# Decoder step on one core: conditioning rows turned by VectorE, position products as 16 products behind the third page unit, pages transposed two units ahead

## The reference

```python
def adaln(c, w_ada, b_ada):
    mod = jax.nn.silu(c) @ w_ada + b_ada
    return jnp.split(mod[:, None, :], 6, axis=-1)

def compress(rows, pe, w1, w2):
    ...
    proj = jnp.einsum('bnkf,rfh->rbnkh', chunks, w1.reshape(r_n, CMP_STRIDE * HEAD_DIM, CMP_HIDDEN))
    pre = sum(proj[r][:, r:r + nc] for r in range(r_n)) + pe.reshape(-1) @ w1
    out = jax.nn.silu(pre) @ w2
```

## Time and profile before

| | us |
|---|---|
| median of 3 runs | 924.52 |
| lowest and highest | 923.3, 925.25 |
| the profiled execution | 924.75 |
| its span, first to last instruction | 922.9 |
| PE busy in the span | 854.2 (93%) |
| DVE busy | 622.8 (67%) |
| ACT busy | 372.8 (40%) |
| POOL busy | 307.5 (33%) |

### The profile page before, as it was taken

The page is one execution under the profiler, slowest core; times in us unless marked ns, Lnnn a source line. Parts: engine busy times, 40 slices in busy tenths (PEclk is TensorE's granted clock), DMA queues, the critical chain, the costliest instruction groups (busy, mean ns, idle before and its releaser), DMA issues.

```text
span 922.9 us, 17110 instructions
## 1 busy us (share of the span) xinstructions
PE 854.2 (93%) x6689; PEld 733.0 (79%) x6689; DVE 622.8 (67%) x1219; ACT 372.8 (40%) x751; POOL 307.5 (33%) x303
## 2 busy tenths in 40 slices
PE   3498999999988789899999998999999999999998
PEld 2366778899976556676777798999999999888886
DVE  2156585388945775758486899888888888434444
ACT  1033252141234343767843664444444446223221
POOL 6465400000003321535500318777766773000000
PEclk9699999999988788999999999999999999999999
DMA  7988913236276798294102453333333324422201
GB/s 207 344 306 313 317 47 99 94 110 243 68 263 249 277 376 301 51 316 138 36 1 92 129 147 107 98 101 104 95 93 93 93 92 153 156 92 92 74 1 52
DMA packets 89166, 138.88 MB, mean 150 GB/s; under 512 B 9267, under 2 KB 59987, under 8 KB 84798
## 3 DMA queue, kind: packets, MB, share of 16 engines
q1 hardware_dynamic: 74866, 96.26, 32.6%
q0 software_dynamic: 9376, 40.31, 12.2%
q10 hardware_dynamic: 4844, 1.21, 0.6%
HBM read 130.58 MB, written 11.31 MB: 154 GB/s over the span
## 4 chain that ended last, share of the span: by engine, by line
PE 78%; DVE 8%; issue 7%; ACT 3%; another core or an unknown queue 1%; POOL 1%; DVEq 0%; ACTq 0%; POOLq 0%
PE bank L2438 18%; PE bank L2440 18%; PE bank L2439 18%; PE bank L2432 4%; PE bank L2506 4%; PE bank L2794 2%; PE bank L2708 2%; PE bank L2926 2%; PE bank L2467 2%; PE bank L2448 2%; PE bank L2447 2%; PE bank L2958 2%; PE bank L2764 1%; DVE mem L1602 1%
## 5 line engine op out<-in xcount | busy, mean ns | idle before, releaser
L2438 PE MATMUL bank<-s,ring_hi 128*128 128x288 f32 x620 | 184.7, 298 | 3.7 <-DVE ring_lo L536 3.7
L2439 PE MATMUL bank<-s,ring_lo 128*128 128x288 f32 x620 | 183.6, 296 | 0.0
L2440 PE MATMUL bank<-s,ring_hi 128*128 128x288 f32 x620 | 183.0, 295 | 0.0
L2438 PEld LDWEIGHTS bank<-s,ring_hi 128*128 128x128 f32 x620 | 116.8, 188 | 4.6 <-DVE ring_lo L536 4.5
L2440 PEld LDWEIGHTS bank<-s,ring_hi 128*128 128x128 f32 x620 | 117.5, 190 | 0.0
L2439 PEld LDWEIGHTS bank<-s,ring_lo 128*128 128x128 f32 x620 | 117.0, 189 | 0.0
L536 DVE TENSOR_TENSOR ring_lo<-mem,ring_hi 128x512 fp32r<-128x512 f32 x84 | 106.3, 1301 | 2.1 <-POOL mem L988 1.8
L536 DVE TENSOR_TENSOR dn_w<-wring,dn_w 128x2048 fp32r<-128x2048 f32 (+1 forms) x11 | 23.1, 2096 | 65.9 <-ACT dn_w L533 65.9
L2438 PE MATMUL bank<-dn_w,dn_hi 128*128 128x512 f32 x160 | 62.2, 389 | 0.0
L2439 PE MATMUL bank<-dn_w,dn_lo 128*128 128x512 f32 x160 | 62.2, 389 | 0.0
L2440 PE MATMUL bank<-dn_w,dn_hi 128*128 128x512 f32 x160 | 62.2, 389 | 0.0
(11 more groups left out here) (444 smaller groups left out, 2126.5 us busy)
## 6 DMA issues: line engine op xcount, KB each, us to landing
wring<-in_w_gu SPq DMA_DIRECT2D x44, 512.0 KB
wring<-in_w_ada SPq DMA_DIRECT2D x16, 1024.0 KB
wring<-in_w_in SPq DMA_DIRECT2D x10, 1024.0 KB
wring<-in_w_down SPq DMA_DIRECT2D x10, 1024.0 KB
wring<-in_w_ada SPq DMA_DIRECT2D x16, 512.0 KB
proj<-in_x_prompt SPq DMA_DIRECT2D x4, 512.0 KB
mem<-in_state_k_win POOLq DMA_DIRECT2D x8, 256.0 KB
mem<-in_state_v_win POOLq DMA_DIRECT2D x8, 256.0 KB, 7.5
```

What stands on the lines that cost most here:

```text
L2438: pe.matmul(dst, sh, ml, start=first and k == 0, stop=False)
L2439: pe.matmul(dst, sl, mh, start=False, stop=False)
L2440: ins = pe.matmul(dst, sh, mh, start=False, stop=last and k == len(pairs) - 1)
```

## The change

It does five things.

1. The conditioning rows are loaded in 8 DMAs so that four groups of partitions hold a quarter each (`crow` is 128 by 256 now, cleared by DVE ahead of the load), and after the Silu DVE transposes them in one instruction into `cT`. The 8 products on PE and the copy out of PSUM are gone.
2. The position products use both halves of the weight rows at once: 16 products with 128 columns of weights and two moving columns. DVE adds the two halves that are wanted (a copy and an addition for each of keys and values).
3. On PE the order is unit 0, unit 1, the transpose of the gain rows, unit 2, the position products, and only then `compress_second(0)`. All through the loop `compress_second` stands one unit later: unit u is followed by `compress_second(u - 2)`.
4. DVE transposes pages 0 and 1 ahead of its loop, and in iteration u page u + 2. That page's buffer is the one that PE frees when it has finished unit u.
5. On ACT's queue the loads of the value weights and of the second weights stand ahead of the gain rows.

The diff, cut to its core (the bank list `plan_banks` follows the new order on PE and loses the key `cT`; two semaphores, `c_cleared` and `c_turned`, are new):

```diff
@@ SP
-            sp.dma_start(crow[0:1, :], a["c_prompt"]).then_inc(c_loaded, 16)
-            sp.dma_start(crow[1:9, :], a["c_sample"]).then_inc(c_loaded, 16)
+            sp.wait_ge(c_cleared, 1)
+            for q in range(4):
+                for r0, n, name in ((0, 1, "c_prompt"), (1, 8, "c_sample")):
+                    sp.dma_start(crow[32 * q + r0:32 * q + r0 + n, :].rearrange("b (k r) -> b k r", r=32),
+                                 a[name].rearrange("b (k q r) -> q b k r", q=4, r=32)[q]).then_inc(c_loaded, 16)
@@ ACT
             hidden_load(0)
+            hidden_load(1)
+            for x, w in enumerate(("w_ck2", "w_cv2")):
+                act.dma_start(w2[:, 64 * x:64 * x + 64], a[w][0]).then_inc(comp_w_loaded, 16)
...
-            hidden_load(1)
-            for x, w in enumerate(("w_ck2", "w_cv2")):
-                act.dma_start(w2[:, 64 * x:64 * x + 64], a[w][0]).then_inc(comp_w_loaded, 16)
             act.dma_start(stc, a["state_conv"].rearrange("l b r f -> (l b r) f")).then_inc(conv_state_loaded, 16)
-            act.wait_ge(c_loaded, 32)
+            act.wait_ge(c_loaded, 128)
             act.activation(scrow, crow, ACT.Silu).then_inc(scrow_ready, 1)
@@ def hidden(u), ACT
+                if u < 2:
+                    want_emptied(act, ("peb", u))
@@ DVE
             turn_chunks(0)
+            turn_chunks(1)
             for u in range(16):
-                if u < 15:
-                    turn_chunks(u + 1)
-                if u >= 2:
-                    cmp_evac(u - 2)
-                if u == 0:
-                    evac(("cT",), cT[:, :].rearrange("p (k r) -> p k r", r=32)[:, :, 0:9],
-                         ps(("cT",))[:, 0:72].rearrange("p (k r) -> p k r", r=9))
+                if u < 14:
+                    turn_chunks(u + 2)
+                if u >= 3:
+                    cmp_evac(u - 3)
+                if u == 1:
                     evac(("rows",), colT[:, :], ps(("rows",))[:, 0:52])
+                    dve.wait_ge(scrow_ready, 1)
+                    dve.transpose(cT[:, :], scrow).then_inc(c_turned, 1)
                     for x in range(2):
-                        evac(("peb", x), pebt[:, x:x + 1], ps(("peb", x))[64 * x:64 * x + 64, 0:1])
+                        want_filled(dve, ("peb", x))
+                        link(dve.tensor_copy(pebt[:, 2 + x:3 + x], ps(("peb", x))[64:128, 1:2]))
+                        frees(dve.tensor_tensor(pebt[:, x:x + 1], pebt[:, 2 + x:3 + x], ps(("peb", x))[0:64, 0:1], ALU.add),
+                              ("peb", x))
...
+            cmp_evac(13)
             cmp_evac(14)
@@ def position_rows(), PE
                 for x in range(2):
                     want_free(pe, ("peb", x))
-                ins = [None, None]
-                for i in range(16):
-                    for x in range(2):
-                        ins[x] = pe.matmul(ps(("peb", x))[64 * x:64 * x + 64, 0:1], w1v[:, x, i % 8, i // 8, :], colT[:, 36 + i:37 + i],
-                                           start=i == 0, stop=i == 15)
-                for x in range(2):
-                    fills(ins[x], ("peb", x))
+                    for j in range(8):
+                        ins = pe.matmul(ps(("peb", x))[:, 0:2], w1v[:, x, j].rearrange("p r h -> p (r h)"),
+                                        colT[:, 36:52].rearrange("p (r j) -> p j r", r=2)[:, j], start=j == 0, stop=j == 7)
+                    fills(ins, ("peb", x))
@@ the loop, PE
             for u in range(16):
                 if u == 0:
+                    pe.wait_ge(comp_k_loaded, 128)
+                if u == 1:
+                    pe.wait_ge(comp_w_loaded, 160)
+                compress_first(u)
+                if u == 1:
                     turn_rows()
-                    pe.wait_ge(comp_k_loaded, 128)
-                compress_first(u)
-                if u == 0:
+                if u == 2:
                     position_rows()
+                if u == 4:
+                    pe.wait_ge(c_turned, 1)
...
-                if u:
-                    compress_second(u - 1)
+                if u >= 2:
+                    compress_second(u - 2)
+            compress_second(14)
```

28 lines of the change are left out of this document (11 added, 17 removed).

## The result

The changed kernel takes **944.0 us** (median of four runs, 938.9 to 949.4) where the kernel before takes 924.2 on the same chip: a ratio of **1.022, 95% interval 1.019 to 1.025**. The prediction was 924.7 with a range up to 929.5. The profiled run took 944.12 us with a span of 942.3; the runs of the changed kernel scatter over 10 us, those of before over 2.

A forecast was written before the change was run, and what follows sets the result against it. PE was taken as the bound, busy 93%, so gains must come from its standing still. Terms -4.4 - 1.0 + 3.3 + 1.7 + 0.6 = +0.2 us gave 924.7 against the median of 924.52; range 913.5 to 929.5.

The forecast's parts named there:

- the hold-up: From about 24 to 38.4 us: PE's reports of finished matmuls held back under a certain kind of memory traffic.
- That rival: First part: gathers feed the hold-up, PE held until 42, 3.5 us later, 928; 21 in 100 shared with another case.
- the hold-up stays: First part, likeliest case: the hold-up lasts as long as before, kernel at 924.7 us; 42 in 100.
- The position products: Behind unit 2: 32 passes with 128-wide weights take 3.5 us, bounds 1.9 to 4.1, ending at 44.5.
- A gain of 4.4: Up to unit 3: it starts at 45.2, against 50.42, less 0.8 for the clock; range 2 to 5.2.
- The second stage's slack: In the units: `compress_second` a unit later avoids PE's 2.20 us wait behind ACT's Silu; gain 1.0, from 0 to 2.2.
- The tail: From iteration 12 to the input projection: the new order adds waits of 3.3, 1.7 and 0.6, together 5.6 us.
- Its first term: Iteration 12: page 14's transpose waits for unit 12 ahead of the modulation addition, so PE stands; +3.3 us.
- Its second: Iteration 13: page 15's transpose waits for unit 13 and stands ahead of the modulation, so PE waits; +1.7 us.
- Its third: Input projection: its fourth tile waits for unit 15's PSUM bank; +0.6 us, from 0 to 1.4.
- The hold-up gone: First part, rival: two full units in place of the small passes clear the hold-up, -9 us, 915.5; 18 in 100.
- The recorder: Rival: PE stands because profiling records can't be written, so only the tail's 5.6 counts, 930 us; 2 in 100.

The follow-up runs named there:

- the run with the products behind unit 0: Changed kernel with the gain rows' transpose put back ahead of unit 0 and the 16 wide position products behind unit 0; 923.2 us, 1.014 to the kernel before.
- the lead alone: Kernel before with only pages turned two units ahead and second stages two units behind; 938.1 us, ratio 1.016 to the kernel before.
- after again: The changed kernel, unedited, profiled again beside the kernel before where that showed no first hold-up; 925.4 us, ratio 1.014 to the kernel before.
- page 6 held back: Changed kernel with POOL gathering page 6 only once page 3 is turned; 941.1 us, ratio 1.018 to the kernel before.
- the tail mended: Changed kernel with DVE writing modulation rows and columns ahead of the page transposes of iterations 12 and 13; 940.3 us, 1.013 to the kernel before.

## Why the prediction was wrong

**What bounds the kernel** was read rightly in what it saw and wrongly in what it made of it. The reports are held back, and the position products only stand there: in the trace of after no product stands behind unit 0, and unit 1's report is 18 us late all the same. But the prediction took the hold-up for fixed, "as long as before", though it had the right rule among its rivals: POOL's last gather by 34.2, release at 38.4, and page 6 now without the pause. That rival was given less than 21 in 100 beside 42 for "the hold-up stays". The step that failed is *"If the hold-up lasts as long as before, unit 1 is reported at 38.4"*: it was reported at 43.57. The rival's own price, 3.5 us for a release at 42, was too low by 1.6.

**The position products** were the second step: 3.5 us, bounds 1.9 to 4.1, measured 6.99. The lower bound came from passes with 64 weight columns at a granted clock of 0.50, the upper from eight passes of 0.127 us each, for which the prediction took a low clock too. The profile gives them a granted clock of 1.00 (15.94 to 16.96 us), and 0.127 us lies near the 0.113 that a wide pass takes at the full clock in the run with the products behind unit 0 (32 in 3.6 us), not near the 0.218 measured at 0.50. So 3.5 was the price at 2.4 GHz for a place that the sum itself put behind 14 us of standing still. With both, unit 3 was forecast at 45.2 and came at 53.99: 5.2 from the release, 3.5 from the products, 0.1 other. A gain of 4.4 became a loss of 3.6.

**The second stage's slack**, -1.0: PE's wait for the Silu, 2.20 us in the earlier trace rows, did go. From unit 3 to unit 5 the changed kernel takes 11.4 us and before 11.7, although unit 3 itself runs at the lower clock for 5.69 us and not 3.72; of the clock, for which the sum gave back 0.8, this is 2.0. From unit 5 to unit 12 it loses 3.1 us instead: the later hold-ups fall elsewhere (in after, PE waits 3.57 us at 79.29, ahead of unit 7); this share varies between runs and no run isolates it.

**The tail** was right in its mechanism and short in its size: forecast 5.6, measured 7.9 to 9. Its first term, 3.3, is 3.27 us of waiting in after, in the lead alone, and in after again. Its second, 1.7 behind unit 13, is 1.3: from the end of unit 13 to the projection 10.9 us, before 9.6. Its third, 0.6 for the bank of the fourth tile, was small: where the tiles ahead ran at the full clock, PE waits 1.16 us there (with page 6 held back, and with the tail mended), since the sum of unit 15 follows ACT's copy, and that stands behind 3.34 us of modulation as it did before. In after itself the low clock stretches those tiles (0.63 us for 0.39) and hides that wait: from the projection's start to the last second stage 5.2 us, before 3.7. Missing altogether was what a wait of TensorE draws behind it: unit 13 runs at the lower clock for a part (5.41, 6.60, 5.60 us for 3.72, at a mean granted clock of 0.68, 0.55 and 0.65), at least 1.7 us more each time.

**That the whole kernel gains or loses what the start of the input projection does** held within 3 us in most kernels (794 to 800 us from there to the end), but after had 803.2 and the tail-mended one 804.8, both with a granted clock of 0.57 in the 20 us beginning 249 us behind the projection's start, where the others have 0.85 to 1.00 (before 1.00). That is some 5 us of the first result that no part of the sum speaks of. Whether an earlier shift makes it likelier can't be told: it came in 2 of 10 profiles of kernels with the lead and in none of 10 others, which chance gives as well.

**The other rivals.** The hold-up gone: not by the change, but it exists as a condition of the chip. The recorder: nothing speaks for it, since where the hold-up stood the profiled run's time lies among those of the timed ones.

## What to carry to other kernels

Before pricing a move that lets one engine run on, ask which queue its progress feeds: here page 2, turned early, put off a pause of POOL that had ended the hold-up. A prefetch of one more stage moves the wait on a buffer's release to the head of an in-order engine's list, and whatever short, late-needed work stands behind it (here the modulation rows) is then late by the whole turn; put such work ahead of the wait. And where a wait of TensorE is added, price the matmuls behind it at the clock that rows behind a like wait show.

## What the hardware showed that was not expected

Completion reports of TensorE can come 15 to 18 us after the matmuls have run while indirect gathers are issued one behind the other, and were let go 3.8 to 6.1 us behind the start of the last one, in eight profiles; meanwhile waiting passes may come singly, with gaps of up to 2.94 us. With at most four gathers under way no late report was seen on the same chip, but such gaps, up to 1.13 us. On other occasions the same kernel shows none of it, with the same gathers and the same DMA share, and is 11 to 13 us faster. By its number, one chip was in both conditions in two groups, one after the other. What sets the condition was not found, and no run could look at it: it stays open.

32 passes with 128 weight columns and two moving columns took 3.63 us at the full clock (products behind unit 0, 25.51 us) and 6.99 at the lower; 64 passes with 64 weight columns and one took 2.03 at the full and 61 of them 3.47 at the lower:

```profile
25.51 3.63 PE L2498 MATMUL bank<-colT,mem 128*128 128x2 f32 x32
```

So half as many, twice as wide products cost 1.8 to 1.9 times as much. The two forms differ in weight columns and in moving columns, and no run separates the two.
